# Fourteen column sums of the modulation moved from the FFN loops into the norms, and a last norm with fewer and wider operations

## The chip, the cores and the metric

The kernel runs on one core of a Trainium2 chip. The time is device microseconds from launch to end; the figure quoted is the median of several runs. The core's engines are TensorE (PE, matrix products into the PSUM memory), VectorE (DVE), ScalarE (ACT), GpSimd (POOL) and SyncE (SP, which issues nearly all transfers). Each runs its own instruction stream; they wait for each other by semaphores.

## What is computed

Two blocks of a network run one after the other on 256 tokens of width 1024, in float32. Everything that matters here is in these lines of the reference, cut down:

```python
# first block, two layers; nine modulation vectors a layer come out of one product
mods = split(silu(c) @ ada_w[layer] + ada_b[layer], 9)          # 1024 x 9216
h = rms_norm(x, g) * (1 + scale) + shift                        # ahead of every sublayer
x = x + 0.5 * (1 + gate) * (silu(h @ w_g) * (h @ w_u)) @ w_out  # an FFN, four in all, d_ff 2816
x = x + (1 + gate) * pool_mixer(h, pool_w, pool_scale)          # layer 0
k, v = kv(rms_norm(x, kv_norm) modulated by silu(c) @ kv_ada_w) # between the layers
x = x + (1 + gate) * attention(q(h), k, v) @ w_o                # layer 1
# second block
shift, scale, gate = split(c_2 @ w_ada + b_ada, 3)
merged = sigmoid(gl_s) * ssm_branch + sigmoid(gl_m) * latent_attention_branch
out = merged @ w_out
x = x + gate * (out * rsqrt(mean(out * out) + eps) * g_post)    # the last norm
```

## The kernel before

**Layout.** x lies transposed, as eight tiles of 128 features by 256 tokens. A float32 weight unit (128 x 1024, 512 KB) is loaded by SP, ACT casts it into a high part `w_hi` (line 355), DVE subtracts that for a low part `w_lo` (line 359), and PE multiplies high by high, high by low and low by high (lines 367 to 369, `products`). Four units are in flight; 391 pass in all.

**An FFN.** Its 22 hidden tiles j each take three weight units: gate, up and out. PE does `gate_unit(j)`, `up_unit(j)` and then `out_unit(j-1)`. Tiles 2 to 21 run in loops of four tiles, given by `SEGMENTS`: in the first three FFNs one loop of five turns, in the fourth five loops of one turn.

**The modulation.** The multiply-adds of `c @ ada_w` are done by DVE: a block `b` of 512 output columns (46 blocks, 2 MB each, loaded into two alternating buffers `g_land`) is summed over eight slices into an accumulator `g_acc[:, b % 2]` of 128 x 512 (`g_part`, lines 1361 and 1364). What is left is the sum over the 128 partitions: `reduce_block(b)` (line 524) has PE multiply four 128 x 128 quarters by a column of ones into four columns of the PSUM bank `mods`. In the FFN loops two blocks are made per turn; `reduce_block` stands between `up_unit` and `out_unit` of every second tile. The semaphore `g_done` counts finished accumulators, `g_red` reduced ones. An accumulator is written again when the block two before has been reduced.

**A norm.** ACT squares the eight tiles of x (line 1027), PE sums them over the partitions with a matrix of ones (`sum_squares`, line 534), ACT takes the root (line 1031), DVE the reciprocal (`root`, line 1407), then DVE scales the eight tiles (line 1417), ACT adds the shift and rounds to `x_hi` (line 1045), DVE makes `x_lo` (line 1424), and PE begins the next products as the tiles come (`first_units`, lines 557, 559, 564). Meanwhile DVE turns columns of `mods` into the coefficients: `gate_coef` (lines 1389 to 1393) and `norm_coef` (1400 to 1403), each after waiting for `g_red` to reach `blocks[0]`. After the first FFN, DVE also runs `gate_coef(1)` and four parts of block 15 ahead of `root(1)`. After the fourth FFN PE runs 128 small state products (`lag_step`, line 875) between the sum of squares and the next products.

**The last norm.** The eight tiles of `out` are evacuated by ACT (line 1100) to `o_raw` and squared from there (line 1336). PE sums all eight squares after its last column (`sum_squares(7)`), ACT roots (line 1338), DVE inverts, and then eight times scales one tile (line 1884) and adds it to x (line 1888). SP stores each of the eight tiles, 128 KB, as its sum is ready.

Of the kernel before, what the change touches and what calls it, by code (L numbers as in the profile page):

```python
# [116 lines left out]
GATES = [(_name, _n) for _name in ("glm", "brm", "zs", "gls") for _n in range(KT)]  # L117

# [19 lines left out]
def build_program(nc, stream, gstream, vecs_d, cons_d, mask2_d, band_d, xin, pos_d, ssm_bw, ssm_bn, ssm_c, out):  # L138
    with ExitStack() as ctx:
# [46 lines left out]
        g_acc = region(32, [2, GW])  # L186
        silu_b = region(36, [2, T])
# [90 lines left out]
        x_upd = sem("x_upd")  # L278
        sq_done, nrm_done, rt_done = sem("sq_done"), sem("nrm_done"), sem("rt_done")
# [21 lines left out]
        base_done = sem("base_done")  # L301
# [6 lines left out]
        done_sem = {"used": used, "part": part_done}  # L308

# [70 lines left out]
        def _(sp):  # L380
# [131 lines left out]
            for k in range(KT):  # L512
                sp.wait_ge(fin_done, k + 1)
                sp.dma_start(out[:, k], x[:, k]).then_inc(out_st, 16)
            sp.wait_ge(out_st, 16 * KT)
# [3 lines left out]
        def _(pe):  # L519
            def reduce_block(b, i=0):  # L520

                pe.wait_ge(g_done, i * 2 + (b + 1))
                for q in range(4):
                    m = nc.tensor.matmul(mods[:, bass.ds(i * 8 + (4 * b + q), 1)],  # L524
                                         g_acc[:, b % 2, q * P:(q + 1) * P], ones[:, 0:1], start=True, stop=True)
                m.then_inc(g_red, 1)

            def sum_squares(n):
# [6 lines left out]
                m.then_inc(nrm_done, 1)  # L535

# [75 lines left out]
            def ffn(f, stage, hi=x_hi, lo=x_lo):  # L612
# [14 lines left out]
                for reps, vector in SEGMENTS[f]:  # L627
                    with pe.Fori(0, reps) as i:
                        for m in range(4):
# [5 lines left out]
                            if vector and m % 2 == 1:  # L635
                                reduce_block(b + m // 2, i)
# [87 lines left out]
            sum_squares(1)  # L724
            for q in range(2):
# [25 lines left out]
            sum_squares(3)  # L751

# [21 lines left out]
            sum_squares(4)  # L774
            def q_unit(h):
# [90 lines left out]
            sum_squares(6)  # L866

# [137 lines left out]
            sum_squares(7)  # L1005
# [3 lines left out]
        def _(act):  # L1009
# [317 lines left out]
            nc.scalar.copy(x_hi[:, 7], gel_at(7)).then_inc(xh_done, 1)  # L1327
            for n in range(KT):
# [13 lines left out]
        def _(dve):  # L1342
# [10 lines left out]
            def g_part(b, k, vector, i=0):  # L1353

                cv = csil[:, k:k + 1] if vector == "silu" else vec("c2", k)
                acc, rows = g_acc[:, b % 2], g_land[:, b % 2, k]
                if k == 0:
                    dve.wait_ge(g_landed[b % 2], i * 16 + 16 * (b // 2 + 1))
                    if b >= 2:
                        dve.wait_ge(g_red, i * 2 + (b - 1))  # L1360
# [35 lines left out]
            def norm_coef(stage):  # L1396
# [6 lines left out]
                link(V.tensor_tensor(coef[:, stage, 8:16], mods[:, sh:sh + 8], vec("bias", sh, 8), ALU.add))  # L1403
# [68 lines left out]
            def ffn(f, stage, pre, gate_col, ahead_units, next_stage):  # L1472
# [26 lines left out]
                blocks[0] = b  # L1499
# [11 lines left out]
                norm_coef(next_stage)  # L1511
                split_lo(dve, ahead_units[2])
# [24 lines left out]
            gate_coef(1, 40, vec("pool_scale", 0, 8))  # L1537
# [4 lines left out]
            norm_t(1)  # L1542
            for k in range(4, 8):
# [337 lines left out]
            ahead(KT)  # L1881
            root(7)
            for k in range(KT):
                V.scalar_tensor_tensor(out=t_buf[:, k], in0=o_raw[:, k], scalar=coef[:, 8, k:k + 1], in1=rx,
                                       op0=ALU.mult, op1=ALU.mult).then_inc(t_done, 1)
                if k:
                    dve.wait_ge(t_done, KT * N_STAGES + k)
                    V.tensor_tensor(x[:, k - 1], x[:, k - 1], t_buf[:, k - 1], ALU.add).then_inc(fin_done, 1)
            dve.wait_ge(t_done, KT * N_STAGES + KT)
            V.tensor_tensor(x[:, 7], x[:, 7], t_buf[:, 7], ALU.add).then_inc(fin_done, 1)  # L1890
# [288 lines left out]
```

## Time and profile before

| | |
|---|---|
| median of 3 runs | 1452.31 us (1451.8 to 1453.49) |
| the profiled execution | 1457.6 us, span 1455.8 us, mean granted PE clock 0.964 |
| busy share PE, DVE, ACT, POOL | 92%, 77%, 43%, 11% |
| DMA | 318 MB, mean 218 GB/s |

The span runs from the first to the last instruction; 1.8 us of the profiled execution's time lie outside of it. The four FFNs take 52 to 249, 288 to 485, 563 to 760 and 868 to 1063 us of the span. A clock of 1.00 is 2.4 GHz on PE, 0.50 is 1.2 GHz.

### The profile page before, as it was taken

To read this page: it belongs to the slowest core of one execution; us is meant where nothing else is said; L and a number is where in the kernel's file an instruction comes from. 1 tells how busy PE (TensorE), PEld (TensorE's weight loads), DVE (VectorE), ACT (ScalarE), POOL (GpSimd) and SP (SyncE) were. 2 spreads that over 40 slices of the span, in tenths; PEclk is the share of its full clock that TensorE was granted. 3 is DMA by queue.
4 is the path that set the end of the run, shared out by engine and by line. 5 is a ranking of instruction groups with operands and counts; after the bars stand their busy time and mean duration, and the time that the engine had idled before them with its cause. 6 is when DMAs were issued, how large, how long until landed. Compare 5 with 4: busy or idle time off the path is not lost.

```text
span 1455.8 us, 28146 instructions
## 1 busy us (share of the span) xinstructions
PE 1337.4 (92%) x10988; PEld 1297.0 (89%) x10988; DVE 1118.1 (77%) x1697; ACT 625.0 (43%) x948; POOL 163.0 (11%) x209
## 2 busy tenths in 40 slices
PE   3899999799999897999998889999996898999996
PEld 2799998799999877999998779999996787999996
DVE  6898777797777787877777657899965777886573
ACT  3333334433333534333344553433364456355443
POOL 6891000000000020000001000000001002331000
PEclk9899999799999998999999899999998999999998
DMA  9788787278876455887753237886655278455551
GB/s 368 258 333 298 288 289 273 90 276 313 289 288 232 128 175 200 338 303 289 290 156 114 71 143 279 342 293 232 210 160 150 78 152 145 140 174 182 166 186 47
DMA packets 91286, 318.06 MB, mean 218 GB/s; under 512 B 21920, under 2 KB 34496, under 8 KB 85056
## 3 DMA queue, kind: packets, MB, share of 16 engines
q1 hardware_dynamic: 91200, 316.87, 63.7%
q8 instruction: 59, 0.97, 0.3%
q14 instruction: 27, 0.22, 0.0%
HBM read 311.82 MB, written 5.01 MB: 218 GB/s over the span
## 4 chain that ended last, share of the span: by engine, by line
PE 76%; DVE 12%; ACT 5%; issue 4%; DMA 1%; POOL 1%; SPq 0%; DVEq 0%; ACTq 0%; POOLq 0%
PE tiles L367 16%; PE tiles L369 15%; PE tiles L368 15%; PE acc L367 6%; PE acc L369 6%; PE acc L368 6%; ACT w_hi L355 2%; PE mods L524 2%; DVE arena L1364 2%; DVE w_lo L359 2%; PE nrm L534 1%; PE tiles L557 1%; PE tiles L559 1%; PE acc L677 1%; DMA land<-in_stream 1%
## 5 line engine op out<-in xcount | busy, mean ns | idle before, releaser
L359 DVE TENSOR_TENSOR w_lo<-land,w_hi 128x1024 fp32r<-128x1024 f32 x391 | 483.0, 1239 | 204.7 <-ACT w_hi L355 202.3
L355 ACT CAST w_hi<-land 128x1024 fp32r<-128x1024 f32 x391 | 408.5, 1046 | 525.6 <-PE tiles L369 286.1
L367 PE MATMUL tiles<-x_hi,w_hi 128*128 128x256 f32 x1464 | 419.3, 286 | 7.6 <-ACT arena L1100 3.9
L368 PE MATMUL tiles<-x_lo,w_hi 128*128 128x256 f32 x1464 | 415.0, 283 | 0.0
L369 PE MATMUL tiles<-x_hi,w_lo 128*128 128x256 f32 x1464 | 414.9, 283 | 0.0
L367 PEld LDWEIGHTS tiles<-x_hi,w_hi 128*128 128x128 f32 x1464 | 281.6, 192 | 11.5 <-ACT arena L1100 4.1
L368 PEld LDWEIGHTS tiles<-x_lo,w_hi 128*128 128x128 f32 x1464 | 281.6, 192 | 1.1 <-issue 1.0
L369 PEld LDWEIGHTS tiles<-x_hi,w_lo 128*128 128x128 f32 x1464 | 281.5, 192 | 0.0
L1364 DVE SCALAR_TENSOR_TENSOR arena<-arena,csil 128x512 f32<-128x512 f32 x280 | 212.5, 759 | 2.0
L367 PE MATMUL acc<-h_hi,w_hi 128*128 128x256 f32 x704 | 202.3, 287 | 0.3 <-DVE h_lo L1383 0.3
L367 PE MATMUL tiles<-a_hi,w_hi 128*128 128x256 f32 (+1 forms) x656 | 188.9, 288 | 13.7 <-DVE a_lo L1715 12.4
L369 PE MATMUL acc<-h_hi,w_lo 128*128 128x256 f32 x704 | 199.2, 283 | 0.0
L368 PE MATMUL acc<-h_lo,w_hi 128*128 128x256 f32 x704 | 199.1, 283 | 0.0
L368 PE MATMUL tiles<-a_lo,w_hi 128*128 128x256 f32 (+1 forms) x656 | 186.5, 284 | 0.0
L369 PE MATMUL tiles<-a_hi,w_lo 128*128 128x256 f32 (+1 forms) x656 | 186.5, 284 | 0.0
L367 PEld LDWEIGHTS tiles<-a_hi,w_hi 128*128 128x128 f32 (+1 forms) x656 | 125.7, 192 | 15.9 <-issue 12.8
L367 PEld LDWEIGHTS acc<-h_hi,w_hi 128*128 128x128 f32 x704 | 135.1, 192 | 0.4 <-issue 0.4
L368 PEld LDWEIGHTS acc<-h_lo,w_hi 128*128 128x128 f32 x704 | 135.1, 192 | 0.0
L369 PEld LDWEIGHTS acc<-h_hi,w_lo 128*128 128x128 f32 x704 | 135.0, 192 | 0.0
L368 PEld LDWEIGHTS tiles<-a_lo,w_hi 128*128 128x128 f32 (+1 forms) x656 | 125.8, 192 | 0.7 <-issue 0.7
L369 PEld LDWEIGHTS tiles<-a_hi,w_lo 128*128 128x128 f32 (+1 forms) x656 | 125.8, 192 | 0.0
L1100 ACT ACTIVATE arena<-tiles 128x256 f32<-128x256 f32 (+4 forms) x81 | 35.3, 435 | 102.7 <-PE tiles L369 94.8
(328 smaller groups left out, 1680.5 us busy)
## 6 DMA issues: line engine op xcount, KB each, us to landing
land<-in_stream SPq DMA_DIRECT2D x391, 512.0 KB, 4.3
arena<-in_gstream SPq DMA_DIRECT2D x46, 2048.0 KB, 8.8
w_dram<-arena SPq DMA_DIRECT2D x3, 512.0 KB, 6.3
arena<-w_dram SPq DMA_DIRECT2D x6, 256.0 KB, 11.0
x<-in_x_t SPq DMA_DIRECT2D x1, 1024.0 KB, 14.0
arena<-in_ssm_bn SPq DMA_DIRECT2D x1, 1024.0 KB, 5.6
u_dram<-arena SPq DMA_DIRECT2D x1, 1024.0 KB, 5.3
arena<-u_dram SPq DMA_DIRECT2D x8, 128.0 KB, 6.3
```

Of the source, the lines that this page charges most:

```text
L355: nc.scalar.copy(w_hi[:, u % RING], land[:, u % LAND]).then_inc(hi_done, 1)
L359: nc.vector.tensor_tensor(w_lo[:, u % RING], land[:, u % LAND], w_hi[:, u % RING].bitcast(F32), ALU.subtract).then_inc(lo_done, 1)
L367: nc.tensor.matmul(outs, lh, rh, start=first, stop=False, **kw)
L368: nc.tensor.matmul(outs, lh, rl, start=False, stop=False, **kw)
L369: last = nc.tensor.matmul(outs, ll, rh, start=False, stop=end, **kw)
L524: m = nc.tensor.matmul(mods[:, bass.ds(i * 8 + (4 * b + q), 1)], g_acc[:, b % 2, q * P:(q + 1) * P], ones[:, 0:1], start=True, stop=True)
L534: m = nc.tensor.matmul(nrm[:, 0:T], ones, t_buf[:, k], start=(k == 0), stop=(k == KT - 1))
L557: nc.tensor.matmul(outs[c], lh, hi[:, k], start=(k == 0 and not (c and one_bank)), stop=False, skip_group_check=True)
L559: nc.tensor.matmul(outs[c], ll, hi[:, k], start=False, stop=False, skip_group_check=True)
L677: m = nc.tensor.matmul(acc4[:, h, qt * T:(qt + 1) * T], qq[0:parts, 2 * g + h, qt * P:(qt + 1) * P], kk[0:parts, 2 * g + h, :], start=True ...
L1100: nc.scalar.activation(dst, src, func, **kw).then_inc(freed["a"], 1)
L1364: V.scalar_tensor_tensor(out=acc, in0=rows, scalar=cv, in1=acc, op0=ALU.mult, op1=ALU.add).then_inc(g_done if k == 7 else g_step, 1)
```

## The change

It has two parts.

**The sums over partitions.** In the first three FFNs the last four blocks (11 to 14, 23 to 26, 34 to 37) are accumulated into four accumulators of their own (`late_acc`), and `reduce_block` is left out of the loop for them; in the fourth the same holds for blocks 44 and 45, in the old accumulators. PE reduces them in `reduce_later(f)`, right after the `sum_squares` that follows the FFN. It first waits for `coef_done`, a new count of finished `norm_coef`s, since those read the same PSUM bank. As the accumulator's choice has to be fixed per instruction, the loop of five turns becomes one of three and two of one. `gate_coef(1)` needs block 11 and now runs after `norm_t(1)`, not ahead of `root(1)`.

**The last norm.** ACT squares each tile of `out` straight from PSUM and only then evacuates it, multiplied by the coefficient (gate times g_post). DVE adds the first seven squares up as they come, so PE sums two tiles in place of eight, the last of them alone once its square is there. The table for the root is loaded ahead, by an operation on one column. After the reciprocal DVE does three pairs of wide operations (4, 2 and 2 tiles) in place of eight pairs, and SP stores in three pieces (512, 256 and 256 KB).

```diff
-SEGMENTS = [[(5, "silu")], [(5, "silu")], [(5, "silu")], [(1, "silu"), (1, "c2"), (1, "c2"), (1, "c2"), (1, None)]]
+SEGMENTS = [[(3, "silu"), (1, "silu"), (1, "silu")]] * 3 + [
+    [(1, "silu"), (1, "c2"), (1, "c2"), (1, "c2"), (1, None)]]
+LATER = [[11, 12, 13, 14], [23, 24, 25, 26], [34, 35, 36, 37], [44, 45]]
+LATE_ACC = {_b: (_f, _n) for _f, _blocks in enumerate(LATER[:3]) for _n, _b in enumerate(_blocks)}
+LAST = [(0, 4), (4, 6), (6, 8)]
...
+        def acc_of(b):
+            if b in LATE_ACC:
+                return late_acc[:, LATE_ACC[b][1]]
+            return g_acc[:, b % 2]
...
+            def reduce_later(f):
+                pe.wait_ge(coef_done, 2 * (f + 1))
+                for b in LATER[f]:
+                    reduce_block(b)
...
-                            if vector and m % 2 == 1:
+                            if vector and m % 2 == 1 and b + m // 2 not in LATER[f]:
                                 reduce_block(b + m // 2, i)
...
             sum_squares(1)
+            reduce_later(0)
...
             sum_squares(6)
+            reduce_later(3)
...
-            sum_squares(7)
+            pe.wait_ge(rt_done, 7)
+            pe.wait_ge(sq_sum, KT - 2)
+            nc.tensor.matmul(nrm[:, 0:T], ones, t_buf[:, 0], start=True, stop=False)
+            pe.wait_ge(sq_done, KT * 8)
+            nc.tensor.matmul(nrm[:, 0:T], ones, t_buf[:, KT - 1], start=False, stop=True).then_inc(nrm_done, 1)
...
+            nc.scalar.activation(eps_root, con("eps", 1), ACT.Sqrt)
             for n in range(KT):
                 ahead()
                 act.wait_ge(af_done, 12 + n + 1)
                 nc.scalar.copy(a_hi[:, n], mrg[:, n]).then_inc(ah_done, 1)
             for n in range(KT):
-                evacuate(TILE["out"] + n, tile_of("out", n), o_raw[:, n])
+                wait_tile(act, TILE["out"] + n)
+                nc.scalar.square(t_buf[:, n], tile_of("out", n)).then_inc(sq_done, 1)
+                evacuate(TILE["out"] + n, tile_of("out", n), o_raw[:, n], ACT.Identity, scale=coef[:, 8, n:n + 1])
                 ahead()
-                wait_freed(act, TILE["out"] + n)
-                nc.scalar.square(t_buf[:, n], o_raw[:, n]).then_inc(sq_done, 1)
...
-            gate_coef(1, 40, vec("pool_scale", 0, 8))
             dve.wait_ge(base_done, 1)
...
             norm_t(1)
+            gate_coef(1, 40, vec("pool_scale", 0, 8))
...
+            for n in range(1, KT - 1):
+                dve.wait_ge(sq_done, KT * 7 + n + 1)
+                V.tensor_tensor(t_buf[:, 0], t_buf[:, 0], t_buf[:, n], ALU.add).then_inc(sq_sum, 1)
+                dve.wait_ge(sq_sum, n)
             root(7)
+            for n, (a, b) in enumerate(LAST):
+                V.tensor_tensor(o_raw[:, a:b], o_raw[:, a:b], rx.unsqueeze(1).to_broadcast([P, b - a, T]),
+                                ALU.mult).then_inc(t_done, 1)
+                dve.wait_ge(t_done, KT * N_STAGES + n + 1)
+                V.tensor_tensor(x[:, a:b], x[:, a:b], o_raw[:, a:b], ALU.add).then_inc(fin_done, 1)
```

## Rows read from the trace of the kernel before

**Rows 1.** The page of the kernel before, its chain of work that ended last, by engine.

```profile
PE 76%; DVE 12%; ACT 5%; issue 4%; DMA 1%; POOL 1%; SPq 0%; DVEq 0%; ACTq 0%; POOLq 0%
```

**Rows 2.** Windows of two FFN tiles: length, busy PE PEld DVE ACT POOL, clock, DMA, GB/s.

```profile
314.40:332.57 18.17, 18.17 (x155) 18.17 (x154) 16.10 (x23) 7.91 (x9) 0.00 (x0) 1.00 0.79 308
...
1011.60:1029.80 18.20, 18.20 (x154) 18.20 (x153) 16.99 (x23) 6.86 (x8) 0.00 (x0) 1.00 0.61 191
```

**Rows 3.** Timeline of PE about one block's sums in an FFN: start, us, engine, line.

```profile
223.29 0.95 PE L524 MATMUL mods<-cons,arena 128*128 128x1 f32 x8
224.10 0.36 PE L367 MATMUL acc<-h_hi,w_hi 128*128 128x256 f32 x1
224.30 0.28 PE L368 MATMUL acc<-h_lo,w_hi 128*128 128x256 f32 x1
```

**Rows 4.** Timeline of the norms after the second, third and fourth FFN.

```profile
486.03 0.17 DVE L1403 TENSOR_TENSOR coef<-mods,vecs 128x8 f32<-128x8 f32 x1
...
491.97 0.55 PE L557 MATMUL tiles<-x_hi,w_hi 128*128 128x256 f32 x1 [3.50 <-ACT x_hi L1045]
...
767.07 0.36 PE L557 MATMUL acc<-x_hi,w_hi 128*128 128x256 f32 x1 [3.50 <-ACT x_hi L1045]
...
1069.79 0.36 PE L557 MATMUL tiles<-x_hi,w_hi 128*128 128x256 f32 x1 [1.10 <-ACT x_hi L1045]
```

**Rows 5.** Timeline of the norm after the first FFN, ahead of the pooling.

```profile
251.09 0.16 DVE L1389 TENSOR_TENSOR coef<-mods,vecs 128x8 f32<-128x8 f32 x1
...
251.49 0.49 DVE L1361 TENSOR_SCALAR arena<-arena,csil 128x512 f32<-128x512 f32 x1
...
254.25 1.75 DVE L1407 RECIPROCAL arena<-arena 128x256 f32<-128x256 f32 x1
...
260.23 0.55 PE L367 MATMUL acc<-w_hi,x_hi 128*128 128x256 f32 x1 [6.86 <-DVE x_lo L1424]
```

**Rows 6.** Busy time and PE clock in two slices of the same norm and pooling.

```profile
255.60:257.20 1.60, 0.00 (x0) 0.00 (x0) 1.56 (x4) 0.65 (x2) 0.00 (x0) 0.57 0.00 0
...
265.20:266.80 1.60, 1.60 (x12) 1.60 (x11) 0.28 (x1) 1.08 (x2) 0.00 (x0) 0.73 0.51 92
```

**Rows 7.** Timeline of PE at the start, the sums of the first block.

```profile
15.24 1.84 PE L524 MATMUL mods<-cons,arena 128*128 128x1 f32 x8 [15.24 <-DVE arena L1364]
```

**Rows 8.** Timeline of the last norm, by engine PE, ACT and DVE in turn.

```profile
1441.45 3.61 PE L534 MATMUL nrm<-arena,cons 128*128 128x256 f32 x16
...
1441.65 0.38 ACT L1100 ACTIVATE arena<-tiles 128x256 f32<-128x256 f32 x1 [2.04 <-PE tiles L369]
1442.07 0.42 ACT L1336 ACTIVATE arena<-arena 128x256 f32<-128x256 f32 x1
1442.50 1.28 ACT L1338 ACT_TABLE_LOAD   x1
1445.11 0.48 ACT L1338 ACTIVATE arena<-nrm,cons 128x256 f32<-128x256 f32 x1 [1.32 <-PE nrm L534]
...
1445.61 1.75 DVE L1407 RECIPROCAL arena<-arena 128x256 f32<-128x256 f32 x1 [12.82 <-ACT arena L1338]
...
1452.92 0.42 DVE L1890 TENSOR_TENSOR x<-x,arena 128x256 f32<-128x256 f32 x1
```

**Rows 9.** Groups of DVE instructions by shape: xcount, busy us, mean ns, idle before.

```profile
L1461 DVE TENSOR_TENSOR arena<-arena,ssm_s 128x1024 f32<-128x1024 f32 x5 | 6.1, 1220 | 0.0
...
L1465 DVE TENSOR_TENSOR arena<-arena 128x512 f32<-128x512 f32 x5 | 3.4, 686 | 0.0
```

**Rows 10.** DMA issues by line: count, KB each, median us from issue to landing.

```profile
out_t<-x SPq DMA_DIRECT2D x8, 128.0 KB, 1.9
...
u_dram<-arena SPq DMA_DIRECT2D x1, 1024.0 KB, 5.3
```

**Rows 11.** Timeline where the last product, out, begins its third tile.

```profile
1423.65 0.38 ACT L1100 ACTIVATE arena<-tiles 128x256 f32<-128x256 f32 x1 [4.87 <-PE tiles L369]
...
1424.08 0.39 PE L367 MATMUL tiles<-a_hi,w_hi 128*128 128x256 f32 x1
```

More of the change, by code:

```diff
@@ L300, in build_program @@
         qrot_done, qrope_done = sem("qrot_done"), sem("qrope_done")
-        base_done = sem("base_done")
+        base_done, coef_done = sem("base_done"), sem("coef_done")
         tab_done = sem("tab_done")
@@ L308, in build_program, with acc_before @@
         done_sem = {"used": used, "part": part_done}
+        def acc_of(b):
+            if b in LATE_ACC:
+                return late_acc[:, LATE_ACC[b][1]]
+            return g_acc[:, b % 2]
+        def acc_before(b):
+            if b in LATE_ACC:
+                f, n = LATE_ACC[b]
+                return LATER[f - 1][n] if f else -1
+            same = [o for o in range(b % 2, b, 2) if o not in LATE_ACC]
+            return same[-1] if same else -1
         def wait_tile(eng, o):
@@ L511, in _ @@
                 load_unit(sp, u, u % LAND)
[L512 to L515, printed above, removed]
+            for n, (a, b) in enumerate(LAST):
+                sp.wait_ge(fin_done, n + 1)
+                sp.dma_start(out[:, a:b], x[:, a:b]).then_inc(out_st, 16)
+            sp.wait_ge(out_st, 16 * len(LAST))
         @block.tensor
@@ L524, in reduce_block @@
                     m = nc.tensor.matmul(mods[:, bass.ds(i * 8 + (4 * b + q), 1)],
-                                         g_acc[:, b % 2, q * P:(q + 1) * P], ones[:, 0:1], start=True, stop=True)
+                                         acc_of(b)[:, q * P:(q + 1) * P], ones[:, 0:1], start=True, stop=True)
                 m.then_inc(g_red, 1)
@@ L774, in _ @@
             sum_squares(4)
+            reduce_later(2)
             def q_unit(h):
@@ L1402, in norm_coef @@
                                             in1=vec(gname, g0, 8), op0=ALU.add, op1=ALU.mult))
-                link(V.tensor_tensor(coef[:, stage, 8:16], mods[:, sh:sh + 8], vec("bias", sh, 8), ALU.add))
+                V.tensor_tensor(coef[:, stage, 8:16], mods[:, sh:sh + 8], vec("bias", sh, 8),
+                                ALU.add).then_inc(coef_done, 1)
+                dve.wait_ge(coef_done, stage + 1)
             def root(n):
@@ L1881, in _ @@
             ahead(KT)
-            root(7)
[L1883 to L1890, printed above, removed]
+            dve.wait_ge(sq_done, KT * 7 + 1)
+            for n in range(1, KT - 1):
+                dve.wait_ge(sq_done, KT * 7 + n + 1)
+                V.tensor_tensor(t_buf[:, 0], t_buf[:, 0], t_buf[:, n], ALU.add).then_inc(sq_sum, 1)
+                dve.wait_ge(sq_sum, n)
+            root(7)
+            for n, (a, b) in enumerate(LAST):
+                V.tensor_tensor(o_raw[:, a:b], o_raw[:, a:b], rx.unsqueeze(1).to_broadcast([P, b - a, T]),
+                                ALU.mult).then_inc(t_done, 1)
+                dve.wait_ge(t_done, KT * N_STAGES + n + 1)
+                V.tensor_tensor(x[:, a:b], x[:, a:b], o_raw[:, a:b], ALU.add).then_inc(fin_done, 1)
         @block.gpsimd
```

12 lines of the change are left out of this document (8 added, 4 removed).

## The prediction, written before the changed kernel ran

> **What bounds the kernel.** I read the chain of waits first. PE is 76% of it [rows 1], and in the order of time its FFN stretches are products alone, with the eight instructions of one `reduce_block` among them once in 18.17 us. Next come windows over one such period. In the second FFN PE is busy 18.17 of 18.17 us and DVE 16.10; late in the fourth it is 18.20 against 16.99 [rows 2]. So in the loops PE is the bound and nothing else: an instruction taken from its stream there shortens the end by its own length, until DVE binds. The timelines of the norms show the opposite: PE waits 3.50 us for the first high tile after the second FFN and again after the third, 1.10 us after the fourth, since `lag_step` fills part of that one [rows 4], and 6.86 us after the first FFN [rows 5]. There ACT and DVE are the bound. The end is a chain: sum of squares, root, reciprocal, eight pairs on DVE, a store [rows 8].
>
> **The 14 reductions leave the loops.** A reduction starts at 223.29 and the next product at 224.10; the one behind that comes at 224.30 [rows 3]. Without it the two would stand at 223.29 and 223.41, as products follow each other every 0.12 us (18.17 us hold 144 products, 144 x 0.12 = 17.28, and 0.89 for the reduction). So one costs 224.30 - 223.41 = 0.89, or 0.81 if the slow first product behind it stays. I take 0.89, since the period agrees: 14 x 0.89 = 12.5 us, and 11.3 as the lower bound.
>
> What must keep pace: a period of two tiles becomes 17.28 us. DVE's 16.10 and 16.99 fit [rows 2], ACT has 7.9, and the transfers' share of 0.79 becomes 0.83.
>
> **The reductions arrive in the norms.** They start when `sum_squares` ends; the wait for `coef_done` costs nothing, as `norm_coef` ends at 486.20, 2.3 us before PE is done with the squares at 488.47 [rows 4]. Four take 4 x 0.81 = 3.25 us, in gaps of 6.86, 3.50 and 3.50 us [rows 4, 5]. Two take 1.6 us in the last gap, which has 1.10 [rows 4]: `lag_step` ends late and the next products start 0.5 us late. Those are paced by ACT's high tiles, one in 0.41 us for two products of 0.12 each, so PE catches up within three tiles. I count 0 and keep 0.5 as the bound. Behind PE in this queue stand only those first products; ACT, which waits for the sum of squares, is released before the reductions.
>
> The cover in the second and third gap is thin: 0.25 us. If it goes, each tenth that the reductions run over is a tenth of the total.
>
> **`gate_coef(1)` moves.** It took 251.49 - 251.09 = 0.40 us ahead of DVE's block parts, and `root(1)` began at 254.25 when those were done [rows 5]. DVE had no idle time ahead of it: the sum of squares ended at 253.37 (260.23 - 6.86 [rows 5]) and ACT's root takes 0.48 [rows 8], so that was ready near 253.9, and `root(1)` starts some 0.3 us earlier. Behind `norm_t(1)` the 0.40 us lie in time in which DVE waits for the pooling products. The sum gets -0.3.
>
> **The split loops.** Three turns and two bodies written out in place of five turns. The fourth FFN is written out already and its PE never waits in [rows 2]; I count 0.
>
> **The last norm.** Term by term [rows 8]:
> - PE. Now 16 passes from 1441.45 to 1445.06, 0.22 us each. After: ACT squares the last tile from PSUM at 1441.65 in about 0.42 us (its evacuation from PSUM took 0.38, a square from SBUF 0.42), and PE adds two passes with some 0.15 us of latency behind it, which ends near 1442.7. The first pair and DVE's six sums (under 0.5 us each, one in 2.9 us) are done before. Gain 2.35. The table load of 1.28 us now lies at 1442.50 beside PE; were it not moved it would end at 1443.8 and leave 1.3 of the gain. It moves to a place where ACT waits for PE to release weight buffers. If the table had to be loaded again all the same, 1.3 is the lower bound of the gain.
> - Root and reciprocal stay: 0.48 and 1.75.
> - DVE's pairs. Now from 1447.36 to 1453.34, 5.98 us. After: two operations of 1024 columns at 1.22 and four of 512 at 0.69 [rows 9] are 5.20, with 0.15 for the five waits in between 5.35. Gain 0.6. The bounds are 0.2 and 0.8: the waits between may cost up to 0.1 each, or nothing.
> - The last store is 256 KB, not 128. A store of 128 KB lands in 1.9 us and one of 1024 KB in 5.3 [rows 10], so 3.4 / 896 x 128 = 0.5 us more. The bounds are 0 and 1.
> - A new cost at the start of `out`. Its first two tiles end nearly together; PE begins the third at 1424.08, when ACT has evacuated the first, begun at 1423.65 [rows 11]. Now a square comes ahead of the evacuation: 0.4 us on PE's path (bounds 0.3 and 0.5). Later tiles don't feel it, each taking 2.9 us.
>
> Sum of the last norm: -2.35 - 0.6 + 0.5 + 0.4 = -2.05.
>
> **Sum.** -12.5 - 0.3 - 2.05 = -14.85 us, against the profiled span of 1455.8: 1440.95, and 1442.75 with the 1.8 us outside of it. That execution was 5.3 us above the median, so I take the difference over to the median: 1452.31 - 14.85 = 1437.4. With every term at its poor end it is -11.3 for the loops, -0.2 for `root(1)`, and in the last norm and `out` -1.3 - 0.2 + 1.0 + 0.5 = 0.0; with the late start of 0.5, 1441.3. With all at the good end, -12.5 - 0.4 - (2.35 + 0.8 - 0.3), it is 1436.6.
>
> **Rivals.**
>
> *The clock stays up.* In the gap after the first FFN the clock falls near 255.8 (the slice from 255.60 has 0.57) and rises near 266.06 (0.73 in the slice from 265.20) [rows 6]. PE works at the low level from 260.23 [rows 5] to there, 5.8 us for work of 2.9. It fell while PE did nothing. With the reductions PE works on until 256.6 and rests 3.3 us in place of 6.86, and in the two shorter gaps only 0.25 us. If it then doesn't fall, up to 2.9 us come back here, and perhaps 0.5 at each of the two others, where ACT's pace hides most of it: 1437.4 - 3.9 = 1433.5. For it: the gap is filled. Against it: the row for such work alone, the first block's, stands at 1.84 us for what takes 0.81 in the loop [rows 7], so it ran at half speed, and no row shows these products holding the clock up. Chance 0.15.
>
> The Trainium skill, "TensorE: Matmul & The Clock Gate", section "Why this matters for your kernels", asks for no idle gaps between bursts of matmuls, or the clock is halved. By that rule this rival is what the change does; the fall in the empty gap agrees with it [rows 6], and whether one-column products count is in no row.
>
> *The reductions run over the gap.* If the clock falls as it did, 2.4 us after the last sum of squares (253.37 to 255.8), the last 0.85 us of the reductions run at half speed: 8 passes at 0.23 [rows 7] are 1.9 us, and they end 4.3 us after the squares, 0.8 over the gap of 3.50. Twice that is 1.6, and a late start in the fourth adds up to 0.5: 1439 to 1439.6. Were all of them at the low level, 4 x 1.84 = 7.4 us in gaps of 3.50, it is 3.9 twice, 0.5 after the first FFN and 2 x 1.84 + 0.5 - 1.6 = 2.6 after the fourth: 1448.3. Chance 0.17, nearly all for the small form.
>
> *DVE becomes the bound.* Its 16.99 us leave 0.29 of a period of 17.28 [rows 2]. If its waits fill that in every such period, about 0.5 of each 0.89 is lost, 7 us over all 14: 1444.4. Against it: only the fourth FFN is that tight. Chance 0.05.
>
> *Part of the last norm does nothing:* the table is loaded again, or the store costs 1 us. 1438.5 to 1440. Chance 0.06.
>
> *Slower.* The bodies written out have to be loaded. Six more are entered than before. The gain of 14.85 is gone, and 2.9 more, when each entry stops PE for 17.75 / 6 = 3.0 us. The fourth FFN enters five such bodies and shows PE busy all through a stretch of them [rows 2], which speaks against even a tenth of it. At 3.5 us each it gives 1458. Chance 0.02.
>
> **Numbers.** The forecast has 0.55; with the rivals' 0.15, 0.17, 0.05, 0.06 and 0.02 that is all. A measurement of this kernel tells 0.2%, 2.9 us, from no change. All cases but the last lie beyond it on the fast side; I give 0.02 to the space between. Faster 0.96, same 0.02, slower 0.02. The range takes in the clock that stays up and the small overrun, and leaves out the large overrun, DVE as the bound and most of the poorest ends together, some 0.12: 1433.5 to 1440.8.
>
> **What the profile after would show.** Right: in the last two turns of FFN one to three, periods of 17.28 us without line 524; 32 passes of it right behind `sum_squares`, over before the first high tile; that tile's products no later than 3.5 us after the squares; `root(1)` 0.3 us earlier; about 1.1 us from the last column to the end of the last sum of squares; six DVE operations after the last reciprocal, 5.35 us. Wrong: passes of 0.23 us in the gaps (overrun), a clock of 1.00 through them (gain beyond mine), PE waits for `w_lo` in the shortened periods, or PE idle where a written-out body begins.

## The result: 1440.72 us, 11.9 us less than before, where 14.9 were forecast

The changed kernel took 1440.72 us (median of 4 executions, 1440.24 to 1442.33) and the kernel before 1452.6 (4 executions). The ratio is 0.992, interval [0.9903, 0.9937]. It is faster, as forecast, but by some 3 us less, and just inside the upper end of 1440.8; twelve later executions of the same kernel, below, have medians of 1442.73 and 1442.58, outside of it. Two slow executions, one of the kernel before (1508.08 us) and one of norm_only (4770.74 us), are left out of all means below.

The page of the changed kernel, the chain of work that ended last, by engine, to be read beside [rows 1]:

```profile
PE 79%; DVE 11%; ACT 5%; issue 3%; DMA 1%; POOL 1%; DVEq 0%; SPq 0%; ACTq 0%; POOLq 0%
```

PE is still the bound. The windows over one period of two tiles, in the second and in the fourth FFN of the changed kernel (columns as in [rows 2]):

```profile
310.00:327.28 17.28, 17.28 (x147) 17.28 (x147) 14.21 (x21) 7.16 (x9) 0.00 (x0) 1.00 0.87 330
1000.00:1017.28 17.28, 17.28 (x146) 17.28 (x146) 16.96 (x23) 6.88 (x8) 0.00 (x0) 1.00 0.63 198
```

PE is busy 17.28 of 17.28 us in both, beside DVE's 16.96 in the tighter one: the shorter period holds. The reductions now stand in the pause, here PE's timeline behind the second FFN (start, us, engine, line):

```profile
481.81 0.38 PE L557 MATMUL nrm<-arena,cons 128*128 128x256 f32 x1
482.03 3.92 PE L547 MATMUL mods<-cons,arena 128*128 128x1 f32 x32
485.81 0.56 PE L586 MATMUL tiles<-x_hi,w_hi 128*128 128x256 f32 x1
```

PE works through: the sums end where the product on the first high tile begins, 485.81. That is 3.62 us after the end of the sum of squares (481.81 + 0.38) where [rows 4] have 3.50. The reductions fill the pause and run over it by 0.1 us at most.

The end of the changed kernel, all engines, to be read beside [rows 8]:

```profile
1427.22 0.59 PE L1040 MATMUL nrm<-arena,cons 128*128 128x256 f32 x2
1427.42 0.38 ACT L1372 ACTIVATE arena<-tiles 128x256 f32<-128x256 f32 x1 [2.13 <-PE tiles L392]
1427.70 0.47 ACT L1137 ACTIVATE arena<-tiles,coef 128x256 f32<-128x256 f32 x1
...
1427.86 0.70 PE L1042 MATMUL nrm<-arena,cons 128*128 128x256 f32 x2
1428.60 0.47 ACT L1376 ACTIVATE arena<-nrm,cons 128x256 f32<-128x256 f32 x1 [0.43 <-PE nrm L1042]
1429.17 1.75 DVE L1447 RECIPROCAL arena<-arena 128x256 f32<-128x256 f32 x1 [3.71 <-ACT arena L1376]
1430.96 1.22 DVE L1930 TENSOR_TENSOR arena<-arena 128x1024 f32<-128x1024 f32 x1
1432.22 1.22 DVE L1933 TENSOR_TENSOR x<-x,arena 128x1024 f32<-128x1024 f32 x1
1433.36 0.68 DVE L1930 TENSOR_TENSOR arena<-arena 128x512 f32<-128x512 f32 x1
...
1435.41 0.69 DVE L1933 TENSOR_TENSOR x<-x,arena 128x512 f32<-128x512 f32 x1
```

The first line on PE is 1427.22 where it was 1441.45, and the reciprocal begins 1.95 us behind it, against 1445.61 - 1441.45 = 4.16. DVE's six operations take 1436.10 - 1430.96 = 5.14 us, against 5.98.

So the loops' period, the pauses behind the second FFN and the end came as forecast. What is missing lies elsewhere, and the profiled executions can't be subtracted to find it: 1457.6 us of before is 5.3 over its median, 1440.7 of after is at its median.

### The profile page after: what moved, and what is told of

It reads as the page before. It is cut to its first block, busy times and chain, and to the rows that moved or that the text cites. A ratio compares the mean times of both kernels' runs of the same rounds, so it can differ in the third digit from the quotient of the medians.

```text
span 1438.9 us, 27599 instructions
## 1 busy us (share of the span) xinstructions
PE 1333.2 (93%) x10976; PEld 1294.4 (90%) x10976; DVE 1118.8 (78%) x1693; ACT 624.8 (43%) x949; POOL 163.2 (11%) x209
## 4 chain that ended last, share of the span: by engine, by line
PE 79%; DVE 11%; ACT 5%; issue 3%; DMA 1%; POOL 1%; DVEq 0%; SPq 0%; ACTq 0%; POOLq 0%
PE tiles L390 16%; PE tiles L392 16%; PE tiles L391 16%; PE acc L390 6%; PE acc L392 6%; PE acc L391 6%; ACT w_hi L378 2%; PE mods L547 2%; DVE arena L1402 2%; DVE w_lo L382 2%; PE nrm L557 2%; PE tiles L586 1%; PE tiles L588 1%; PE acc L706 1%; DMA land<-in_stream 1%
## 5 line engine op out<-in xcount | busy, mean ns | idle before, releaser
L390 PE MATMUL tiles<-a_hi,w_hi 128*128 128x256 f32 (+1 forms) x656 | 188.5, 287 | 13.7 <-DVE a_lo L1756 12.1
L547 PEld LDWEIGHTS mods<-cons,arena 128*128 128x128 f32 x368 | 48.2, 205 | 28.5 <-issue 16.3
```

The costliest lines, as they stand in the source:

```text
L390: nc.tensor.matmul(outs, lh, rh, start=first, stop=False, **kw)
```

## A second quantity: the time at the low clock level

The granted clock has two levels, 1.2 and 2.4 GHz. Each execution comes with its mean clock, and (1 - clock) x 2 x span is its time at the low level: 0.966 over 1438.9 us is 98 us. It differs between executions of one kernel, 84 to 105 us in 90 of the kernel before. Within the executions of one kernel (fitted over all 210 of this study, each kernel about its own mean), each us at the low level goes with 0.28 us of time (standard error 0.02). So a kernel's mean time can be read at equal low time too, as an estimate: the fit is not the same everywhere, 0.36 (error 0.03) in the 90 executions of the kernel before, 0.20 (0.03) in the 120 of all others, 0.15 (0.05) in the 16 of the changed kernel, and that time follows low time within one kernel does not show that low time which an edit adds or removes has the same price. All kernels of the study, in the order in which they ran; the difference is that of mean times to 1453.9, the mean of the kernel before over five of the six comparisons, and the last column takes out 0.28 us for each us of low time over 93.1:

| kernel | median, us | ratio, interval | executions | difference of means | low level, us | at equal low level |
|---|---|---|---|---|---|---|
| before, beside the others | | | 78 | | 93.1 | |
| after | 1440.72 | 0.992 [0.9903, 0.9937] | 4 | -12.9 | 93.5 | -13.0 |
| before_again | 1453.42 | 0.9999 [0.9986, 1.0012] | 12 | +0.4 | 93.2 | +0.4 |
| sums_only | 1446.15 | 0.995 [0.9933, 0.9968] | 6 | -7.9 | 101.6 | -10.2 |
| norm_only | 1451.4 | 0.999 [0.9978, 1.0001] | 11 | -1.9 | 92.8 | -1.8 |
| after_again | 1442.73 | 0.9926 [0.9911, 0.9942] | 6 | -10.9 | 101.8 | -13.3 |
| split_only | 1450.32 | 0.9972 [0.9959, 0.9985] | 12 | -3.3 | 93.0 | -3.3 |
| sums_quarter | 1443.07 | 0.9916 [0.9894, 0.9938] | 6 | -11.0 | 101.8 | -13.5 |
| unit_first_parts_behind | 1439.27 | 0.9894 [0.9872, 0.9916] | 6 | -14.9 | 93.4 | -15.0 |
| warm | 1437.96 | 0.9882 [0.986, 0.9904] | 6 | -15.9 | 81.4 | -12.6 |
| delay_1 | 1442.98 | 0.9926 [0.991, 0.9943] | 6 | -10.7 | 98.5 | -12.2 |
| delay_2 | 1443.0 | 0.9916 [0.9896, 0.9935] | 6 | -11.9 | 97.5 | -13.1 |
| warm_two | 1437.87 | 0.9896 [0.9878, 0.9914] | 5 | -15.3 | 89.7 | -14.3 |
| unit_first | 1440.66 | 0.9907 [0.989, 0.9923] | 5 | -13.1 | 95.5 | -13.8 |
| later_first | 1450.36 | 0.9972 [0.9959, 0.9984] | 12 | -3.9 | 96.5 | -4.9 |
| later_middle | 1447.3 | 0.9955 [0.9937, 0.9973] | 6 | -6.2 | 100.7 | -8.4 |
| later_fourth | 1446.9 | 0.996 [0.9944, 0.9976] | 8 | -6.1 | 89.6 | -5.1 |
| after_third | 1442.58 | 0.9919 [0.9902, 0.9937] | 6 | -11.5 | 98.9 | -13.2 |
| unit_first_parts_behind_again | 1438.49 | 0.9905 [0.9892, 0.9919] | 5 | -15.4 | 94.8 | -15.9 |
| best2 | 1436.27 | 0.9892 [0.9877, 0.9907] | 4 | -16.8 | 86.8 | -15.0 |

The kernel before was not equally fast in all comparisons. It stood at 1452.6 us beside the first four executions of after and at 1451.9 beside the last two kernels, so the difference beside it is -11.6 for after, -13.5 for unit_first_parts_behind_again and -14.8 for best2; for the others it is within 0.6 us of the one in the table. The three sets of the changed kernel then give 11.6, 11.0 and 11.6.

Over its 16 executions the changed kernel stands at 1442.2 us and 98.6 of low time: 11.7 us under before, and 13.2 at equal low time, if the 5.5 us more cost 5.5 x 0.28 = 1.5 us; at the 0.15 of its own executions it would be 0.8.

## The experiments

**Both kernels again, and each half alone.** norm_only has the last norm of after in the kernel before. sums_only is after with the last norm of before: `sum_squares(7)` on all eight tiles, each tile evacuated and then squared, eight pairs on DVE, eight stores, and the root's table loaded where it was.

> The unchanged kernel once more, for a second profile of it. The first profiled execution took 1457.6 us, 5 over the median of 1452.3. Theory A (that execution was an unlucky one, and the change is worth 12 us, not the 17 by which the two traces differ): this profile's span is near 1450.5 us, and the stretch from the third to the fifth FFN-side norm, that is from the sum of squares after the third FFN to that after the fourth, is some 1.4 us shorter than the 302.7 of the first profile. Rival B (the spans of such a profile are always 5 us over the timed ones): a span near 1455.8 again. The ratio to the kernel before is 1.000 within 0.2%.

> The changed kernel once more, beside the others on one chip: -11.9 us, and the two parts' differences should add up to it within 0.7 us. If the parts add up to 14 and the whole stays at 12, they get in each other's way.

> The kernel before with the last norm of the changed one; the sums over partitions stay in the loops. The traces of before and after give -2.2 for PE and root, -0.8 for DVE's pairs, +0.3 for the store and +0.45 for the start of out: -2.3 us. If the missing 3 us lie in the last norm it is near +0.7.

> The changed kernel with the last norm of before: only the fourteen sums over partitions are moved. Theory A (the first FFN gives only three of its four 0.89 back, the others all): -0.89 x 13 - 0.3 = -11.9 us. Theory B (the whole change measures -11.9, so a part of about 3 us is missing somewhere in the FFNs, and the last norm gives 2.3): -9.6 us. Rival C (the sums give the 12.8 of the prediction and the last norm loses): -12.8.

The halves give -1.9 and -7.9 us. The last norm does what it was to do, within its error; the sums fall short of 12.8 by nearly 5, and 2.6 at equal low time, and of all three values that were expected. Together the halves give 9.8 where the whole gave 10.9 beside them, 1.1 apart and not within 0.7; six executions of sums_only, whose mean has an error of 1.0, can't tell this from a sum that holds.

The second profile of the kernel before settles less than was hoped: its execution took 1458.9 us, the slowest of its twelve (1451.18 to 1458.9), and its span 1457.1, not 1450.5. Both profiled executions of this kernel lie at the slow end of its spread, so a stage is judged below over many kernels and not by before against after.

**The written-out loops alone, and each group of blocks alone.**

```
-LATER = [[11, 12, 13, 14], [23, 24, 25, 26], [34, 35, 36, 37], [44, 45]]
+LATER = [[], [], [], []]                                         split_only
+LATER = [[11, 12, 13, 14], [], [], []]                           later_first
+LATER = [[], [23, 24, 25, 26], [34, 35, 36, 37], []]             later_middle
+LATER = [[], [], [], [44, 45]]                                   later_fourth
```

In split_only `gate_coef(1)` also stands where it did before, and in later_middle the accumulator of a third FFN's block waits for the second FFN's alone.

> The changed kernel with no block put off: the loops stay split and written out, all 46 reductions are in them, the new last norm stays. If writing out the loop bodies costs nothing, it stands where the new last norm alone stood, 2 us under the kernel before (about 1451 to 1452), and its mean time at the low clock level is that of the kernel before (about 93 us). If the bodies' loading costs what is missing from the gain (some 3 us over six more entries), it is at or above the kernel before, 1453 to 1455.

> The changed kernel with only the first FFN's four blocks put off; the other ten are summed in the loops. Beside the kernel with none put off (1450.3 us): by 0.88 a block it gains 3.5 us; if the second FFN's late first unit holds the end of this FFN, as the trace says, 2.6 us, 1447.7. If putting off raises the time at the low clock level by itself, some of it is here: over 96 us against 93.

> Only the eight blocks of the second and third FFN are put off. By 0.88 a block 7.0 us under 1450.3, 1443.3, at 93 us of low clock; if these are the ones whose pauses or shorter loops cost clock, 100 us or more of it and 1445 to 1445.5.

> Only the two blocks of the fourth FFN are put off: 1.8 us under 1450.3, 1448.5. If DVE is nearly the bound there, or the pause of 1.10 us is too short for them, 1449.3 or more.

> The changed kernel once more, for its time at the low level: the first four executions had 93.5 us of it on average, six later ones 101.8. If it costs clock, this mean stays over 98 us and the time at 1442 to 1443; if the six were chance, it is 93 to 95 us and 1440.7.

The bodies written out cost nothing: split_only is 1.4 us better than norm_only, if anything. Against split_only the groups give, raw and at equal low time: first FFN -0.6 and -1.6, the middle two -2.9 and -5.1, the fourth -2.8 and -1.8. So the first FFN gives less than the 2.6 that was expected even with the late unit, and the middle two less than half of their 7.0; only the fourth gives all of its 1.8 and more. The middle group is where low time comes with it: 100.7 us, all six executions between 98 and 101. The third set of the changed kernel, 98.9 us, is over 98 again; the first set's 93.5 was a mean of four between 83 and 104.

The timelines give the length of each stage. Means over the 17 profiled executions without wide products in the pauses, by whether the blocks of that FFN were put off; an FFN counts from its first hidden tile's activation to the first sum of squares behind it (the two runs with a delay and the three with a changed order are left out of the first FFN's row):

| stage | summed in the loop | put off | difference | forecast |
|---|---|---|---|---|
| first FFN | 194.39 (6) | 191.72 (6) | -2.67 | -3.56 |
| second, third FFN | 193.10 each (6) | 189.56 each (11) | -3.54 each | -3.56 each |
| fourth FFN | 190.47 (6) | 188.08 (11) | -2.39 | -1.78 |
| attention behind the second FFN | 76.19 (6) | 76.92 (11) | +0.73 | 0 |
| attention behind the third FFN, with the norm behind it | 104.06 (6) | 104.39 (11) | +0.33 | 0 |

In the FFNs the table gives 2.67 + 7.08 + 2.39 = 12.1 us, nearly the 12.5 of the forecast; the fourth FFN varies by itself (189.5 to 192.3 us with all blocks summed in the loop, 187.7 to 189.0 with two put off), and its shortest against its shortest is 1.80. In the last two rows the work is the same but for the reductions in the pause. There the mean low time is 13.6 us against 14.9, and 19.9 against 20.2. Windows over the two stages in split_only (length, busy PE PEld DVE ACT POOL, clock, DMA, GB/s):

```profile
488.79:565.43 76.64, 63.95 (x357) 54.78 (x358) 59.19 (x70) 33.63 (x52) 7.97 (x4) 0.91 0.49 177
764.73:857.30 92.57, 77.64 (x536) 72.47 (x536) 57.57 (x132) 48.01 (x105) 5.86 (x8) 0.93 0.30 104
```

and in later_middle:

```profile
485.00:562.89 77.89, 68.18 (x384) 58.96 (x384) 59.19 (x70) 33.63 (x53) 7.97 (x4) 0.89 0.50 176
758.64:853.00 94.36, 83.01 (x563) 76.45 (x562) 57.66 (x132) 48.12 (x105) 5.86 (x8) 0.91 0.30 104
```

Same work but for the reductions (27 more records on PE, in the pause), 1.25 and 1.79 us longer, at a clock of 0.89 against 0.91 and 0.91 against 0.93. A stage of 77.88 or 77.89 us behind the second FFN, with 17.1 us of low time, is in 4 of the 11 profiles with these blocks put off and in none of the 6 without, which chance alone would give once in seven times; the changed kernel by itself has 75.94, 77.89 and 76.76 us there in its three profiles. The later stage has both lengths in both kinds.

**Do the sums in the pauses bring the low time?** They are four passes of one column a block. sums_quarter leaves out three quarters of each sum:

```
                 for b in LATER[f]:
-                    reduce_block(b)
+                    pe.wait_ge(g_done, b + 1)
+                    nc.tensor.matmul(mods[:, bass.ds(4 * b, 4)], acc_of(b)[:, 0:P], ones[:, 0:4], start=True, stop=True).then_inc(g_red, 1)
```

> In the norm pauses each of the 14 blocks is summed with one product of four columns over its first 128 rows, in place of four products of one column over four tiles: three quarters of these sums are left out, so the pauses hold 4 short products and not 16. The theory that the short products in the pauses cost clock says that the time at the low level falls back from about 102 us to about 93 and the run to about 1440 (some 2.8 us under the changed kernel). The theory that they run over the pause says that only the fourth pause can gain, 0.5 us at most. If the low level comes with the shorter loops themselves, nothing changes: about 1442.9 and 102 us.

No: 1442.8 on average and 101.8 us, where after_again stood (1442.9 and 101.8, in another comparison). It also shows that the sums fit the pauses. PE's timeline behind the second FFN in sums_quarter has the pause again, and still the first product comes no earlier by more than 0.1 us:

```profile
482.13 0.81 PE L557 MATMUL nrm<-arena,cons 128*128 128x256 f32 x3
482.77 0.95 PE L565 MATMUL mods<-cons,arena 128*128 128x4 f32 x8
486.44 0.55 PE L587 MATMUL tiles<-x_hi,w_hi 128*128 128x256 f32 x1 [2.72 <-ACT x_hi L1083]
```

From the end of the squares (482.94) to that product it is 3.50 us, as in before, and 3.62 in after.

**Is it where the later stages fall?** delay_1 puts three products into the first FFN of the changed kernel, delay_2 six into that of unit_first_parts_behind (below), one to two at each place from which a reduction was taken:

```
+                            if f == 0 and vector and m % 2 == 1 and b + m // 2 in LATER[0]:
+                                for _ in range([1, 1, 1, 0][b + m // 2 - LATER[0][0]]):
+                                    nc.tensor.matmul(nrm[:, 0:T], ones, cons[:, CON["ident"]:CON["ident"] + T],
+                                                     start=True, stop=True)
```

> The changed kernel with three products of 256 columns, whose result nobody reads, at the places in the first FFN from which reductions were taken: all that follows comes some 1.2 us later, and nothing else differs. If the extra time at the low clock level (98 to 102 us against 93) comes only from where the later stages fall against the moments at which the chip sets its level, this shift, which brings them near the place that they have in the run with the weight unit first, takes it back to about 93 us and gives back what it costs: 1441 to 1443. If the low time belongs to what PE does in the pauses and loops, it stays at 98 to 102 us, and the run is 1.2 us longer than the changed kernel, 1443.5 to 1444.

> The kernel with the weight unit first and the parts behind (1438.9 us, 93 us at the low level) with six such products in the first FFN, about 2.4 us, which puts all later stages back to where the changed kernel has them. If the alignment sets the low time, it rises to about 101 us, and the run to 1438.9 + 2.4 + 2.5 = 1443.8. If not, it is 1441.3 at 93 us.

delay_1 speaks against it: 98.5 us of low time, as the changed kernel has, and its time is 1.0 us over it. delay_2 decides nothing. Its six executions are spread over 86 to 107 us, with a mean of 97.5 against 94.0 for that kernel, and its time lies between the two forecasts.

**The end of the first FFN.** The chain of waits of the changed kernel there (start, us, what):

```profile
235.55 0.33 SPq L408
235.92 8.25 DMA land<-in_stream
244.20 1.05 ACT w_hi L378
245.27 1.28 ACT L1061
...
247.22 3.71 PE nrm L557 x16
250.95 0.48 ACT arena L1068
251.46 1.76 DVE arena L1447
```

In the program of SyncE the second FFN's first weight unit (L372) stands behind that FFN's first modulation block (L408, 2 MB), and the block behind the release of a buffer; they are issued at 235.92 and 235.55. The unit lands at 244.17, ACT has to cast it ahead of the norm's squares, and so this landing, not PE's last product, sets when the norm begins.

It was so in the kernel before too. Its rows there: ACT's cast, PE's last product, and ACT's squares and root:

```profile
246.66 1.05 ACT L355 CAST w_hi<-land 128x1024 fp32r<-128x1024 f32 x1 [2.74 <-DMA land<-in_stream]
...
247.98 0.28 PE L369 MATMUL acc<-h_hi,w_lo 128*128 128x256 f32 x1
...
249.13 2.54 ACT L1027 ACTIVATE arena<-x 128x256 f32<-128x256 f32 x8
253.41 0.47 ACT L1031 ACTIVATE arena<-nrm,cons 128x256 f32<-128x256 f32 x1 [1.73 <-PE nrm L534]
```

and of the changed kernel PE's last product and DVE's last three operations on the block:

```profile
244.80 0.28 PE L392 MATMUL acc<-h_hi,w_lo 128*128 128x256 f32 x1
...
248.96 2.33 DVE L1402 SCALAR_TENSOR_TENSOR arena<-arena,csil 128x512 f32<-128x512 f32 x3
```

Both counted from DVE's first `h_hi` of this FFN (55.55 and 55.91), the last product comes 3.54 us earlier in after, as forecast, but ACT's cast and the squares 2.8, and the reciprocal 3.15, with the 0.3 of `root(1)` in it. In before ACT's root ended at 253.88 and DVE's parts of the block at 254.25, so DVE set the reciprocal, and ACT's chain from the landing was 0.4 us behind it. In after DVE's parts end at 251.29 and ACT's root at 251.42: now ACT's chain sets it, by 0.1. Two edits, first the order alone and then with DVE's parts of the block behind the norm:

```
-                if G_FIRST[f]:
+                if G_FIRST[f] and f != 1:
                     g_load(b)
                     b += 1
                 for u in range(base, base + 5):
                     if not (f == 0 and u < LAND):
                         load_unit(sp, u, u % LAND)
+                    if f == 1 and u == base:
+                        g_load(b)
+                        b += 1
...
-            for k in range(4):
-                g_part(G_POOL, k, "silu")
             root(1)
             norm_t(1)
             gate_coef(1, 40, vec("pool_scale", 0, 8))
-            for k in range(4, 8):
+            for k in range(8):
                 g_part(G_POOL, k, "silu")
```

> The changed kernel with the weight unit loaded ahead of the block alone; DVE does four parts of that block ahead of the pooling norm, as before. If ACT's wait for this unit was what held the squares and DVE's parts then hold root(1), the stretch to the pooling norm's reciprocal shortens by 0.9 us or less; if the transfer alone held it, by the whole 2.4 us that both together gave.

> Two things in which the trace of the changed kernel showed a reduction's gain held back at the end of the first FFN: SyncE loads the second FFN's first weight unit ahead of that FFN's first modulation block, and DVE does all eight parts of the block there behind the pooling norm. If the late transfer and DVE's four parts are what holds root(1), the stretch from the last product of the first FFN to the pooling norm's reciprocal shortens by 0.9 to 1.9 us and so does the run: about 1441 to 1442 against 1442.9. If these are covered by another wait (ACT's own work ahead of the squares) nothing changes.

> The same kernel once more: 1438.9 us if the gain of 3 us over the changed kernel is its own, with 93 us at the low level if the lower low time is its own too; 98 us or more and 1440 to 1441 if that part was chance, which leaves it the 1.8 us that the end of the first FFN gave back.

With the order alone (unit_first) the first FFN lasts 189.64 us up to the squares, 1.9 less than in after, but the reciprocal comes only 0.2 to 0.3 us earlier, for the chain now runs through DVE:

```profile
248.91 1.08 issue
249.98 0.49 DVE arena L1402
250.50 0.76 DVE arena L1405
251.29 0.76 DVE arena L1405
252.08 0.75 DVE arena L1405
252.83 1.68 DVE arena L1450
```

Four operations on the block, 249.98 to 252.83, stand ahead of the reciprocal (L1450), as they did in before [rows 5]. The two waits end nearly together, and whoever takes one away meets the other. With both edits the chain from PE's last product on is ACT, PE, ACT, DVE with no wait for a transfer or for DVE's parts:

```profile
241.76 1.05 ACT w_hi L378
242.84 1.28 ACT L1064
...
244.78 3.71 PE nrm L560 x16
248.51 0.48 ACT arena L1071
249.09 1.76 DVE arena L1450
```

The reciprocal comes 1.8 us earlier than in after, counted from the first `h_hi` (193.70 us in both runs of this kernel, 195.54 to 195.62 in after's three profiles). Both runs give 1438.7 us on average over 11 executions, 3.5 under the changed kernel, or 3.1 with each beside the kernel before of its own comparison, and 2.2 at equal low time. It is faster than both kernels. The trace accounts for 1.8 us of that; the low time, 94.1 us against 98.6, is shorter too, and why is not known.

**Wide products in the pauses.** warm is that kernel with seven products of 256 columns behind the reductions of the pooling norm and behind `sum_squares(2)` and `sum_squares(5)`; warm_two has only the last two; best2 adds that the first tile of out is evacuated first, squared from SBUF and scaled on DVE.

```
+            def keep_warm(n, after=0):
+                for _ in range(n):
+                    nc.tensor.matmul(tiles[:, 1, T:2 * T], ones, cons[:, CON["ident"]:CON["ident"] + T], start=True, stop=True)
...
             sum_squares(2)
+            keep_warm(7)
```

> The kernel of the run before with seven products of 256 columns, whose result nobody reads, put behind the pooling norm's sums and behind the sums of squares of two later norms. If wide products there hold the clock up where the one-column ones did not, the time at the low level falls by up to 10 us in these places, and the run by some 2 to 3 us against the run before it. If they only push the first products of the next stage back, or the clock falls all the same, it is the same or slower by up to 1 us a place.

> As the kernel with wide products in three pauses, without those in the pooling norm's pause, where they ran at half speed and ended behind the first tile. If they only cost time there and hold the clock in the other two, it is 1436 to 1437.5; if their gain came from all three, 1438 to 1439.

> The weight unit first, the parts behind, wide products in the pauses of two norms, and the first tile of out evacuated before it is squared, which DVE then scales: 0.4 us less at the start of out, the scaling hidden beside PE. About 1437.5 to 1438 (0.4 under the run with products in two pauses); 1438.5 if DVE's scaling comes late.

Windows of 9 us over the norm ahead of the second FFN, without these products (unit_first_parts_behind, clock 0.81) and with them (warm_two, 1.00):

```profile
273.50:282.50 9.00, 6.95 (x41) 6.68 (x42) 8.96 (x19) 4.24 (x9) 0.00 (x0) 0.81 0.01 2
```

```profile
274.50:283.50 9.00, 8.45 (x56) 7.26 (x55) 8.96 (x19) 4.72 (x10) 0.00 (x0) 1.00 0.00 1
```

With them the clock stays up, and from the reciprocal to the second FFN it takes 10.22 us in place of 11.13 and 10.82. Within 6 us of the reciprocals of these two norms the clock falls in all 17 profiles without the products, and in none of the 3 with them. The Trainium skill ("TensorE: Matmul & The Clock Gate", section "Why this matters for your kernels") asks for no idle gaps between bursts of matmuls; these windows agree, but the pause that one-column sums fill does not: there the clock fell from 1.00 to 0.50, as the last windows of this document show. In the pooling norm, where the clock had already fallen, they only cost; PE's timeline in warm:

```profile
255.01 5.59 PE L572 MATMUL tiles<-cons 128*128 128x256 f32 x14
260.25 0.47 PE L390 MATMUL acc<-w_hi,x_hi 128*128 128x256 f32 x1
```

That stage takes 24.53 us there and 23.81 in warm_two. In all, 4 to 12 us of low time were saved and the time moved by less than a us: warm_two's mean is 1438.5 against 1438.7. So 0.28 us for each us of low time does not hold for low time that is removed here: warm has 12.7 us less of it and is 0.7 us faster, not 3.6. best2 has the lowest median, 1436.27, and a mean of 1437.1 over 4 executions; its ratio of 0.9892 and the 0.9905 of unit_first_parts_behind_again in the same comparison have overlapping intervals.

## Why the prediction was off by 3 us

Mean against mean, 14.85 us were forecast and 11.7 measured.

- **The step that failed: "14 x 0.89 = 12.5", taken in full for the end.** The price was right: 3.54 / 4 = 0.885 in the second and third FFN. But not all 14 reach the norm behind at it. In the first FFN 2.67 of 3.56 us came: PE's last product was 3.54 us earlier, and the squares waited for ACT, which waited for the landing of a weight unit. The prediction looked at DVE, at ACT and at the share of the transfers within a period, and not at what must be there at the last product. It read [rows 5] as DVE's four parts alone holding `root(1)`, with the root ready 0.35 us before; it did not ask what set that root, which was the landing at 246.66, not PE. Cost: 0.9 us, with the trace. With both holds gone the reciprocal came 1.8 us earlier, more than the change had lost there.
- **The clock's 0 in the sum.** The rival weighed a clock that stays up, and the other direction only for the reductions themselves. What the runs show is 5.5 us more at the low level, an estimated 0.8 to 1.5 us of time; the attention stages behind the pauses are 0.73 and 0.33 us longer. It came with the blocks of the second and third FFN (later_middle), yet unit_first_parts_behind puts them off too and has only 94.1. It isn't the sums in the pauses (sums_quarter), and a shift of all that follows did not take it back (delay_1). What it is stays open.
- **Most of the 3.1 us is not placed.** By the stages the change should give 12.1 us in the FFNs, 0.2 at `root(1)` and 2.3 in the last norm, less 1.1 in the attention stages, where the clock's share would be: 13.5 us. The 0.9 lost in the first FFN is in it, and so is a fourth FFN that gained 0.6 more than forecast. Measured are 11.7, and no timeline shows where the other 1.8 us are; the two means have errors of 0.4 and 0.3. The parts do not add up exactly either: split_only and the three groups give -3.3 - 0.6 - 2.9 - 2.8 = -9.6 raw, and -11.8 at equal low time, against -11.7 and -13.2 for all in one.
- **The reductions in the pauses cost nothing**: right, shown by the timeline and by sums_quarter. The overrun's chance of 0.17 was for something that did not occur.
- **The clock stays up**, a rival with 0.15: it did not. In after the reductions run at 1.00, and the first products behind them at the low level; windows of after, the first within the reductions behind the second FFN, the second behind them, the third behind the fourth FFN:

```profile
482.03:485.20 3.17, 3.17 (x31) 3.17 (x29) 2.43 (x3) 1.56 (x3) 0.00 (x0) 1.00 0.49 165
485.30:488.60 3.30, 3.30 (x17) 3.30 (x17) 3.30 (x10) 3.05 (x8) 0.00 (x0) 0.50 0.00 0
...
1071.60:1075.00 3.40, 3.40 (x31) 3.40 (x30) 1.80 (x2) 2.35 (x3) 0.00 (x0) 1.00 0.24 99
```

  Only in the last pause, where `lag_step` works too, did it stay up: the fall near 1071 of the kernel before is in 3 of 6 profiles with these two blocks summed in the loop and in none of the 14 with them put off.
- **`root(1)` 0.3 us earlier**: the start of the sum of squares to the reciprocal takes 4.24 us in after, 0.2 to 0.3 less than in the two profiles of before.
- **DVE as the bound**: did not happen. The fourth FFN gained 2.4 us, or 1.8 by its shortest stages, not less than 1.8.
- **Written-out bodies**: nothing lost, as counted; 1.4 us may even be gained, in means that are good to about 0.5 each, and no timeline says where.
- **The last norm**: PE -2.2 (forecast 2.35), DVE's operations -0.84 (0.6), the store +0.34 (0.5), the start of out +0.37 (0.4), in sum -2.3 against -2.05; norm_only measured -1.9.

## What to carry to other kernels

Where an engine is the bound in a loop, an instruction taken out is worth its length only up to the next thing that must be in place at the loop's end; look at the last turn for what lands or finishes within a few us of it, on the DMA queue above all, and free it in the same change. When two such waits end together, take away both before judging either. Where a clock changes between levels by itself, record its time at each level for every execution, and compare a kernel with the one before of the same comparison: against one pooled mean three sets of the changed kernel gained 12.9, 10.9 and 11.5 us, beside their own 11.6, 11.0 and 11.6. A price of low time that is fitted within kernels is a help in reading, not a measurement of what an edit does: in warm it was wrong by nearly 3 us.

## What the runs showed of the hardware that was not expected

- Products of one column, each with a full load of weights, filled a pause from 482.03 to 485.81 with PE busy throughout, and the clock fell behind them all the same, from 1.00 to 0.50. Seven products of 256 columns in two other pauses of about 3.5 us kept it at 1.00 (3 profiles); in this same pause wide products were not tried.
- The same kernel has 84 to 105 us at the low level from one execution to the next, and its time follows at 0.36 us for each (0.28 over all kernels).
- A stage of the same work differs from one profile to the next: the attention stage behind the second FFN took 75.94, 77.89 and 76.76 us in three profiles of the changed kernel, with 13.7, 17.1 and 13.7 us at the low level.
